# A pair of attention heads scored on halves and quarters of the array

## What is computed

```
q_pe = apply_rope(q_pe, cos, sin)
k_pe = broadcast_to(apply_rope(k_rope, cos, sin), (B, S, N_HEADS, 32))
qh = concatenate([q_nope, q_pe], -1)          # 64 + 32
kh = concatenate([k_nope, k_pe], -1)
s  = einsum('bhqd,bhkd->bhqk', qh, kh) * 96 ** -0.5
p  = softmax(where(mask, s, neg))
attn = p @ v
```

## Time and profile before

| | us |
|---|---|
| median of 3 runs | 1641.82 |
| lowest and highest | 1636.39, 1643.15 |
| the profiled execution | 1642.61 |
| its span in the trace | 1640.8 |
| PE busy in the span | 1594.1 (97%) |
| heads, 1153.2 to 1181.3: PE busy | 28.10 of 28.10 |
| attention, 1181.3 to 1253.6: PE busy | 69.53 of 72.30 |
| the same stretch: DVE and ACT busy | 50.30 and 50.27 |

### The profile page before, as it was taken

One profiled execution on the slowest core, in us unless ns is written; L12 is line 12 of the kernel. 1 busy time (PEld: TensorE's weight loads), 2 busy tenths in 40 slices (PEclk: granted clock), 3 DMA queues, 4 the chain that ended last, 5 costly groups with the idle time before them and its releaser, 6 DMA issues.

```text
span 1640.8 us, 20921 instructions
## 1 busy us (share of the span) xinstructions
PE 1594.1 (97%) x8638; PEld 1295.0 (79%) x8638; DVE 1158.4 (71%) x1620; ACT 735.6 (45%) x988; POOL 316.9 (19%) x211
## 2 busy tenths in 40 slices
PE   7999999999999999999999999999999998999997
PEld 6778678987888898888888899878756877788885
DVE  6898767947343388733656478969566747999998
ACT  5453652366122343221222244342675336777774
POOL 2011000033000010240000001434101005555651
PEclk9999998999999999999999999999999999999999
DMA  7344237832322424444335432222200108999995
GB/s 306 145 160 154 87 121 191 258 117 81 122 94 90 150 104 180 173 160 179 128 131 181 176 110 78 77 94 86 103 27 26 52 8 328 393 397 396 371 382 194
DMA packets 70657, 271.07 MB, mean 165 GB/s; under 512 B 23969, under 2 KB 32801, under 8 KB 44065
## 3 DMA queue, kind: packets, MB, share of 16 engines
q1 hardware_dynamic: 45392, 163.60, 28.0%
q0 software_dynamic: 15696, 101.87, 15.6%
q10 hardware_dynamic: 9472, 4.26, 1.0%
HBM read 244.29 MB, written 25.41 MB: 164 GB/s over the span
## 4 chain that ended last, share of the span: by engine, by line
PE 68%; DVE 22%; ACT 5%; DMA 2%; POOL 1%; issue 1%; SPq 0%; DVEq 0%; ACTq 0%; POOLq 0%
PE bank L396 67%; DVE wsplit L2908 5%; DVE parts L2908 5%; DMA ring<-in_wmoe,indices 1%; DVE wsplit L1926 1%; ACT wsplit L1177 1%; DVE hidden L2932 1%; DVE gla_state L2252 1%; DVE products_early L2037 1%; DVE hidden L2934 1%; DVE hidden L2930 1%; DVE hidden_low L2921 1%; ACT g_high L1468 1%; DVE block_out L2950 1%; POOL r_row L3020 0%
## 5 line engine op out<-in xcount | busy, mean ns | idle before, releaser
L1926 DVE TENSOR_TENSOR wsplit<-ring,wsplit 128x2048 fp32r<-128x2048 f32 x82 | 191.0, 2330 | 153.3 <-ACT wsplit L1177 153.3
L396 PE MATMUL bank<-h_high,wsplit 128*128 128x512 f32 (+1 forms) x992 | 291.0, 377 | 1.2 <-DVE h_low L2572 1.1
L1177 ACT ACTIVATE wsplit<-ring 128x2048 fp32r<-128x2048 f32 x93 | 177.7, 1912 | 163.5 <-PE bank L396 156.0
L396 PE MATMUL bank<-xn_high,wsplit 128*128 128x512 f32 (+1 forms) x832 | 218.3, 348 | 1.8 <-DVE xn_low L1978 1.8
L396 PEld LDWEIGHTS bank<-h_high,wsplit 128*128 128x128 f32 x992 | 181.2, 188 | 37.5 <-DVE h_low L2572 1.5
L396 PE MATMUL bank<-h_low,wsplit 128*128 128x512 f32 (+1 forms) x496 | 185.0, 373 | 0.0
L396 PE MATMUL bank<-f_high,wsplit 128*128 128x512 f32 (+1 forms) x576 | 170.9, 376 | 0.2 <-DVE wsplit L1926 0.2
L396 PEld LDWEIGHTS bank<-xn_high,wsplit 128*128 128x128 f32 x832 | 146.5, 191 | 23.0 <-DVE xn_low L1978 2.0
L396 PE MATMUL bank<-xn_low,wsplit 128*128 128x512 f32 (+1 forms) x416 | 139.4, 347 | 0.0
L396 PEld LDWEIGHTS bank<-f_high,wsplit 128*128 128x128 f32 x576 | 105.6, 188 | 20.2 <-DVE wsplit L1926 0.4
L396 PEld LDWEIGHTS bank<-h_low,wsplit 128*128 128x128 f32 x496 | 93.5, 188 | 17.4 <-issue 0.2
(11 more groups left out here) (542 smaller groups left out, 3278.5 us busy)
## 6 DMA issues: line engine op xcount, KB each, us to landing
ring<-in_W SPq DMA_DIRECT2D x122, 1024.0 KB, 4.9
weights_out<-prep SPq DMA_DIRECT2D x8, 864.0 KB, 7.1
prep<-weights_out_early POOLq DMA_DIRECT2D x8, 576.0 KB, 3.5
toeplitz<-kpad SPq DMA_DIRECT2D x128, 32.0 KB, 3.2
xslot<-zeros SPq DMA_DIRECT2D x7, 516.0 KB, 5.1
block<-xslot SPq DMA_DIRECT2D x6, 516.0 KB, 11.4
yslot<-block_out SPq DMA_DIRECT2D x6, 512.0 KB, 8.5
prep<-turns_early POOLq DMA_DIRECT2D x8, 288.0 KB, 2.4
```

Source lines behind the costliest of these rows:

```text
L396: return g.matmul(o, l, r, start=first, stop=last_, skip_group_check=True)
L1177: g.activation(split_in(n, 0), ringt[:, n % RING, :], ACT.Copy).then_inc(*a.sig(("high", n)))
L1926: g.tensor_tensor(split_in(n, 1), ringt[:, n % RING, :], hi, SUB).then_inc(*t.sig(("low", n), ("released", n)))
```

## The change

The 64 and the 32 rows are no longer joined. The queries' and keys' 64 rows stay where the projection puts them, two heads in the two halves of 128 partitions: `QN[pr]`, `KN[:, pr, :]`, each copied by ACT in one instruction of 128 partitions per bank tile (4 for the queries and 4 for the keys in place of 8 and 8). The rotated rows are laid out so that each of the four quarters of 32 partitions holds one: `QR[pr]` has head 2pr, head 2pr + 1, head 2pr, head 2pr + 1 (four additions of 64 partitions on DVE for each unit, as many as before), and `KR` has the key four times (four copies of 32 partitions on ACT, between the weight part after `kv` and the keys; POOL's copy is gone).

`scores(pr, hf)` makes tiles m = 2hf and 2hf + 1 of both heads of a pair. It first asks for four banks, then issues four products of 64 rows, alternately on the lower and the upper half, and then four of 32 rows, one on each quarter, which add to the same four banks. Only these signal. DVE's and ACT's orders follow: for each m both heads. The buffers of the ring are numbered the same way, and `soften` waits for the transposes of the head that had the buffer.

```diff
         def probs(h, m):
-            return PB[(4 * h + m) % 10]
+            return PB[(8 * (h // 2) + 2 * m + h % 2) % 10]
...
-            def scores(h):
+            def scores(pr, hf):
...
-                for m in range(4):
-                    b = fresh("s", h, m)
-                    mm(b, QH[0:96, h, 128 * m:128 * m + 128], KH[0:96, h, :], True, True).then_inc(*p.sig(("s", h, m), ("scored", h)))
-                    banks.close("s", h, m)
+                pairs = [(e, 2 * hf + x) for x in range(2) for e in range(2)]
+                grown = [fresh("s", 2 * pr + e, m) for e, m in pairs]
+                for b, (e, m) in zip(grown, pairs):
+                    r = slice(64 * e, 64 * e + 64)
+                    mm(b, QN[pr][r, 128 * m:128 * m + 128], KN[r, pr, :], True, False)
+                for x, (b, (e, m)) in enumerate(zip(grown, pairs)):
+                    r = slice(32 * x, 32 * x + 32)
+                    mm(b, QR[pr][r, 128 * m:128 * m + 128], KR[r, :], False, True).then_inc(*p.sig(("s", 2 * pr + e, m), ("scored", 2 * pr + e)))
+                for e, m in pairs:
+                    banks.close("s", 2 * pr + e, m)
...
-            scores(0)
-            scores(1)
+            scores(0, 0)
+            scores(0, 1)
...
                     turn_probs(h)
-                    if h < 6:
-                        scores(h + 2)
+                    if pr < 3:
+                        scores(pr + 1, h % 2)
...
-                for h in range(4 * i, 4 * i + 4):
-                    j, e = 4 * i + 2 + (h % 4) // 2, h % 2
+                for x in range(2):
+                    j = 4 * i + 2 + x
                     a.wait_ge(*at("uq", j, 0))
-                    g.activation(QH[0:64, h, :], banks.at("uq", j, 0)[64 * e:64 * e + 64, :], ACT.Copy).then_inc(
-                        *a.sig(("free", "uq", j, 0), ("nope_ready",)))
+                    g.activation(QN[2 * i + x], banks.at("uq", j, 0), ACT.Copy).then_inc(*a.sig(("free", "uq", j, 0), ("nope_ready",)))
             next_high("kv", 0)
...
+            a.wait_ge(*at("kpe0"))
+            for r in range(4):
+                g.activation(KR[32 * r:32 * r + 32, :], kpe[64:96, :], ACT.Copy).then_inc(*a.sig(("kpe_ready",)))
+            for j in range(4):
+                a.wait_ge(*at("kh", j))
+                g.activation(KN[:, j, :], banks.at("kh", j), ACT.Copy).then_inc(*a.sig(("free", "kh", j), ("kh_ready",)))
+
+            def soften(pr, hf):
+                for m in (2 * hf, 2 * hf + 1):
+                    for z in range(2):
...
-                for e in range(4):
-                    r = slice(32 * e, 32 * e + 32)
-                    g.tensor_tensor(QH[64:96, 4 * i + e, :], KP[r, 0, :], KP[r, 1, :], ADD).then_inc(*v.sig(("rope_ready",)))
+                for x in range(2):
+                    r = slice(64 * x, 64 * x + 64)
+                    for y in range(2):
+                        g.tensor_tensor(QR[2 * i + x][64 * y:64 * y + 64, :], KP[r, 0, :], KP[r, 1, :], ADD).then_inc(*v.sig(("rope_ready",)))
...
-            def soften(h):
-                z = h % 2
+            def soften(pr):
                 for m in range(4):
-                    n = 4 * h + m
-                    v.wait_ge(*at("s", h, m))
-                    if n > 9:
-                        v.wait_ge(*at("turned", (n - 10) // 4))
+                    for z in range(2):
+                        h = 2 * pr + z
+                        n = 8 * pr + 2 * m + z
+                        v.wait_ge(*at("s", h, m))
+                        if n > 9:
+                            v.wait_ge(*at("turned", 2 * ((n - 10) // 8) + n % 2))
...
             next_low("uq", 0)
-            q.wait_ge(*at("kpe0"))
-            q.wait_ge(*q.own())
-            g.tensor_copy(KH[64:96, :, :], kpe[64:96, :].unsqueeze(1).to_broadcast([32, 8, 512])).then_inc(*q.sig(("kpe_ready",)))
             next_low("uq", 1)
```

More of the change, by code:

```diff
@@ L293, in program @@
         qlh, qll = tile("q_high", 29816, 3, 512, dt=F32R), tile("q_low", 31352, 3, 512, dt=F32R)
-        QH, KH, V2 = tile("qh", 0, 8, 512), tile("kh", 10240, 8, 512), tile("v2", 16896, 4, 512)
+        QN = [tile(f"q_nope{k}", o, 512) for k, o in enumerate((0, 512, 2048, 3072))]
+        QR = [tile(f"q_rope{k}", o, 512) for k, o in enumerate((1024, 1536, 2560, 3584))]
+        KN, KR, V2 = tile("k_nope", 10240, 4, 512), tile("k_rope", 12288, 512), tile("v2", 16896, 4, 512)
         QF = tile("attn", 0, 8, 512, dt=F32R)
@@ L1735, in scalar @@
                     next_high("uq", i)
-                for h in range(4 * i, 4 * i + 4):
-                    j, e = 4 * i + 2 + (h % 4) // 2, h % 2
+                for x in range(2):
+                    j = 4 * i + 2 + x
                     a.wait_ge(*at("uq", j, 0))
-                    g.activation(QH[0:64, h, :], banks.at("uq", j, 0)[64 * e:64 * e + 64, :], ACT.Copy).then_inc(
-                        *a.sig(("free", "uq", j, 0), ("nope_ready",)))
+                    g.activation(QN[2 * i + x], banks.at("uq", j, 0), ACT.Copy).then_inc(*a.sig(("free", "uq", j, 0), ("nope_ready",)))
             next_high("kv", 0)
[L1742 to L1745, removed]
-            def soften(h):
-                z = h % 2
[L1749 to L1752, removed]
+            a.wait_ge(*at("kpe0"))
[8 more added lines that the diff above has]
+                        h = 2 * pr + z
+                        a.wait_ge(*at("shifted", h, m))
+                        g.activation(probs(h, m), probs(h, m), ACT.Exp, bias=st[:, z, m:m + 1], scale=-1.0, accum_out=st[:, z, 4 + m:5 + m]).then_inc(
+                            *a.sig(("exp", h, m)))
             def probs_out(h):
@@ L1763, in scalar @@
                 g.activation(V2[:, m, :], banks.at("v2", m), ACT.Copy).then_inc(*a.sig(("free", "v2", m), ("v2_ready",)))
-            soften(0)
-            soften(1)
+            soften(0, 0)
+            soften(0, 1)
             a.wait_ge(*at("end", "heads", "pe"))
@@ L2693, in vector @@
                 v.wait_ge(*v.own())
-                for e in range(4):
-                    r = slice(32 * e, 32 * e + 32)
-                    g.tensor_tensor(QH[64:96, 4 * i + e, :], KP[r, 0, :], KP[r, 1, :], ADD).then_inc(*v.sig(("rope_ready",)))
+                for x in range(2):
+                    r = slice(64 * x, 64 * x + 64)
+                    for y in range(2):
+                        g.tensor_tensor(QR[2 * i + x][64 * y:64 * y + 64, :], KP[r, 0, :], KP[r, 1, :], ADD).then_inc(*v.sig(("rope_ready",)))
             next_low("kv", 0)
-            def soften(h):
-                z = h % 2
+            def soften(pr):
                 for m in range(4):
-                    n = 4 * h + m
-                    v.wait_ge(*at("s", h, m))
-                    if n > 9:
-                        v.wait_ge(*at("turned", (n - 10) // 4))
-                    g.tensor_tensor_reduce(out=probs(h, m), in0=banks.at("s", h, m), in1=MK[:, m, :], scale=-(96.0 ** -0.5), scalar=-BIG,
-                                           op0=ADD, op1=ALU.min, accum_out=st[:, z, m:m + 1]).then_inc(
-                        *v.sig(("free", "s", h, m), ("shifted", h, m)))
+                    for z in range(2):
+                        h = 2 * pr + z
+                        n = 8 * pr + 2 * m + z
+                        v.wait_ge(*at("s", h, m))
+                        if n > 9:
+                            v.wait_ge(*at("turned", 2 * ((n - 10) // 8) + n % 2))
+                        g.tensor_tensor_reduce(out=probs(h, m), in0=banks.at("s", h, m), in1=MK[:, m, :], scale=-(96.0 ** -0.5), scalar=-BIG,
+                                               op0=ADD, op1=ALU.min, accum_out=st[:, z, m:m + 1]).then_inc(
+                            *v.sig(("free", "s", h, m), ("shifted", h, m)))
             def normalise(h):
```

6 lines of the change are left out of this document (2 added, 4 removed).

## The result

| | before | after |
|---|---|---|
| median of 13 runs each, us | 1641.21 | 1645.1 |
| lowest and highest | 1634.25, 1643.83 | 1642.93, 1647.98 |
| the profiled execution | 1642.61 | 1646.46 |
| its span | 1640.8 | 1644.6 |

The changed kernel takes 1.003 of the time of the one before (95% interval 1.0019 to 1.0042), 3.9 us more. That is no difference at the 0.5% used above, and 1645.6 had been forecast.

The account below looks back on a forecast made before the run. PE, busy 97% of the span, was the bound. Waits of 11.4 us less 3.9 saved in calls and 3.4 of earlier idle time gave +4.1 by table; +3.8 was taken: 1645.6 us against the median, range 1639.0 to 1652.5.

Parts of the forecast that it names:

- Heads: While the heads are made, ACT's changed copies and POOL's dropped copy were to change the time by 0.
- A call: One call of scores on PE was to take 2.95 us instead of 3.44, saving 3.9 us in eight calls.
- The mean's bank: PE's third call of scores was to wait 2.8 us for the bank of the convolution's mean, freed after DVE's centring.
- The fourth bank: Calls after an odd head's transposes were to wait 1.07 us each, three times, for a bank freed by DVE's fourth tile.
- ACT's 0.25 in front of `attend`: `attend` was to wait 0.25 us for ACT's exponentials and copies, three times, 0.75 in all.
- The first wait: In the first pair, PE was to idle 0.56 us before the transposes, waiting for the first normalised tile.
- the third pair's first call: This call of scores was to wait 1.0 us for the first `attend`'s bank, freed after DVE has normalised both heads.
- the 0.17: Two further waits of PE for the first normalised tile, 0.17 us each.
- the projection's 0.2: PE's wait at the output projection was to be 0.2 us, where 1.15 was idle before.
- the first two rivals: Quarters run two at a time, 6.9 us later (0.15, shared with costly shape changes); halves run in turn, some +30 (0.03).
- The third, the gain: Without the waits, only PE's own saving is left: -3.9 us, 1637.9; chance 0.09.
- The fourth, the clock: The wait for the mean's bank may lower PE's clock, costing up to +1.7 us: 1647.3; chance 0.18.

Follow-up runs that it names:

- the first experiment: Changed kernel, with the convolution mean's bank given back only after the third call of scores: 1641.44 us, 1.0001 of before.
- the tiles by head: Both bank edits and ACT's copies first, plus DVE, ACT and ring taking one head's two tiles, then the other's: 1639.77 us, 0.9995 of before.

## Why the prediction was right

**Heads: 0, and it was 0.** PE is busy 28.10 of 28.10 us. ACT's four copies of the rotated key took 2.59 (2.46 forecast) and its four key copies 2.07 (2.46), and the keys were ready 4 us ahead of PE, as these rows of ACT's timeline show:

```profile
1171.55 2.59 ACT L1751 ACTIVATE k_rope<-k_pe 32x512 f32<-32x512 f32 x4
1174.16 2.07 ACT L1754 ACTIVATE k_nope<-bank 128x512 f32<-128x512 f32 x4
```

**A call: 2.95 forecast, 2.98 measured.** Its parts were 1.92 for the halves and 1.07 for the quarters. Two turns and one turn are 1.72 and 0.86, so the changes of shape take 0.41, where 0.37 had been estimated. The Trainium skill (TensorE: Matmul & The Clock Gate, Part 3, Measured speedup vs the span model) has 3.07 for four row tiles, and 1.12 us for this step had been worked out from it. The trace has 3.44 / 1.07 = 3.2 for the group with its change of shape counted in, so the page's figure is near the group as a whole and not the turn alone, whose 3.44 / 0.86 is 4.0. The "some 2 us" by which it would have moved the end did not come.

**The mean's bank: 2.8 forecast, 2.55 measured**, and taking it away (the first experiment) moved the last `attend` by 2.60. This one wait is two thirds of the loss.

**The fourth bank: 3 x 1.07 forecast, 3 x 0.99 measured**, but for another reason than was said. The forecast had the bank freed 5.76 after the call's start, by DVE's pace alone. It was free at 5.95, because DVE's fourth tile waits for the odd head's transposes to give back a buffer of the ring, and the forecast left the ring out; with two quarters at a time the wait is 0.99 again, though DVE's pace would have had it nearly gone. The size came out near by luck: the two chains end 0.19 apart. Nor was its price on the path 3.0: with the mean's bank out of the way, asking for the banks one by one gave 0.50, since ACT was next. The forecast's sum needed no such price, because it worked the rounds out one after the other.

**ACT's 0.25 in front of `attend`: not there.** The copies of the turned tiles were in time, since the call begins 0.19 later than forecast, and `attend` starts with its call's end, 8.94 after the pair's first call (8.96 forecast). The first wait, 0.56 for the first normalised tile, was 0.23; the third pair's first call waited 0.75 instead of 1.0; the 0.17 were 0.18; the projection's 0.2 was nothing. The waits together are 6.9 us instead of 8.9. Most are a little shorter than forecast, by up to 0.33 each, and yet all four `attend`s are where they were forecast to 0.2 us: what I took as waiting of PE is in part fed transposes and the few hundredths between groups, which the timeline counts as work. The places were right but for the ring, and the split was not.

**The sum.** Over the stretch PE idles 4.6 more, saves 8 x 0.46 = 3.7 in the calls, and the difference to 3.86 is 2.9 of longer groups, nearly all fed transposes (2.6 forecast). +3.8 forecast, +3.86 measured. That the sum is right to 0.1 while its terms are off by up to 0.75 (the three waits for ACT together) is in part luck.

**The rivals.** Four quarters turn together, so the first two rivals are out. The price of the first was worked out wrong: "since PE is on the path in all eight calls" fails for two of them, and the price was 5.1, not 6.9. The third, the gain, fell with the banks, and how little is behind it was a surprise: with nearly all of those waits taken away the time was 1.0006 of before. That the demand for banks excludes a gain, as the prediction had it, goes too far: with the banks asked for one by one and ACT's copies first, the time was 0.9978 of before. The fourth, the clock, didn't occur in the two profiles of the changed kernel; in the kernels with two quarters at a time and with the halves not in alternation it did, right behind the same wait, and took 1.6 and 1.7 us, the +1.7 forecast.

## What to carry to other kernels

A group of products that is started together makes its banks due together: before halves or quarters of the array are put to use, look at which bank the group asks for last and who frees it, since one bank that was free in time for its own product cost 2.6 us here as a condition of the whole group. Then look for what frees the engine behind the bank: the wait for the fourth bank hung on a ring of buffers that PE itself empties. Shorter products on the busiest engine are worth what the next engine's order leaves of them: 3.7 us of PE's time became 0.47 at the end, and about three times that came from moving four exponentials on ACT. Work the rounds out one after the other, tile by tile, with every buffer in them; single waits were off by up to 0.33 us here, and the ends were right to 0.2 us.

## What the runs showed of the hardware

Products on different halves of the rows need not be issued in alternation to run together. Issued two lower, two upper, their records start 0.013 us apart and a call takes 2.99; in alternation it is 0.006 and 2.98.

A wait of 2.55 us of PE was followed by the lower of the clock's two levels (1.2 GHz in place of 2.4) for 3.4 us in two of the four profiles that have the wait, at a cost of 1.6 to 1.7 us, and by nothing in the other two. The two with the fall are other kernels (two quarters at a time, halves not in alternation) than the two without (the change, twice), so this alone doesn't show that it is chance. An earlier wait speaks for it: PE idles 2.20 to 2.23 us in front of the products at 90.7 in the earlier trace rows, in code that is the same in every kernel here, and from 88 to 97 us the granted clock was 0.81 in both profiles of the change and in that of ACT's copies first, and 1.00 in all others, before among them.

Such falls lie at other places of every kernel here, and they move whole runs by more than most of the experiments do. From 250 to 268 us the granted clock was 1.00 in the profiles of the mean's bank, of the banks one by one and of the tiles by head; these profiled executions reach their first scores product at 1173.3 to 1173.4 us and took 1635.72, 1637.46 and 1633.67. In all others it was 0.62 to 0.81 there, they reach it at 1177.0 to 1182.9, and took 1640.65 or more. So the 1.1 us by which the first experiment's medians differ more than its stretch has two candidates: a fall behind the wait, which if it came in half of the runs would make up 0.8 (half of 1.6, an estimate), and chance in the falls elsewhere, with which before's own median moved between 1640.95 and 1642.04 from one comparison to the next. Neither was shown.
